# u and y come back in one transfer each, the first conditioning blocks go in four batches, x is split two chunks at a time, powers are built by doubling, and the state inputs move to VectorE

## The reference

```python
mods = (jax.nn.silu(c) @ p['w_ada'] + p['b_ada']).reshape(n, DEPTH, 2, 3, D_MODEL)
h = modulate(x, shift, scale)                 # x * (1 + scale) + shift
u = (h @ w_in).reshape(n, seq, 64, 16)        # 64 groups of 16 channels
a_bar = jnp.exp(lam * dt)                     # 64 complex states a group
b_bar = ((a_bar - 1.0) / lam)[..., None] * lax.complex(b_re, b_im)
bu = einsum('nlgc,gpc->nlgp', u, b_bar)       # bu[:, 0] += a_bar * h0
_, states = lax.associative_scan(_lin_combine, (a_seq, bu), axis=1)
y = gelu(einsum(states, c) + d_skip * u)
z = y @ w_glu
out = z[..., :D_MODEL] * jax.nn.sigmoid(z[..., D_MODEL:])
```

## Time and profile before

| | us |
|---|---|
| median of 3 runs | 2664.37 (2663.33 to 2665.31) |
| the profiled execution | 2662.64 |
| its span in the profile | 2660.8 |
| TensorE busy | 2462.1 (93%) |
| VectorE busy | 1471.5 (55%) |
| GpSimd busy | 1140.3 (43%) |
| ScalarE busy | 626.4 (24%) |
| mean granted TensorE clock | 0.965 of full |

### The profile page before, as it was taken

The page is one execution under the profiler, slowest core; times in us unless marked ns, Lnnn a source line. Parts: engine busy times, 40 slices in busy tenths (PEclk is TensorE's granted clock), DMA queues, the critical chain, the costliest instruction groups (busy, mean ns, idle before and its releaser), DMA issues.

```text
span 2660.8 us, 37232 instructions
## 1 busy us (share of the span) xinstructions
PE 2462.1 (93%) x15472; PEld 2341.2 (88%) x15472; DVE 1471.5 (55%) x2020; ACT 626.4 (24%) x1248; POOL 1140.3 (43%) x604
## 2 busy tenths in 40 slices
PE   5898599879999999999988999987999999999995
PEld 2887499769999999999968999976999999999994
DVE  6998232374565555555574333458555555555555
ACT  4233211143222222122222110103422222222213
POOL 4986234254443434343326333425544444444420
PEclk8999799989999999999999999998999999999998
DMA  6445532102222222112101221100111111111102
GB/s 247 122 125 126 168 111 103 64 16 80 72 80 72 80 79 72 57 63 80 64 32 46 80 72 40 56 25 16 56 48 41 48 48 48 48 48 42 47 24 71
DMA packets 92591, 187.31 MB, mean 70 GB/s; under 512 B 29584, under 2 KB 51856, under 8 KB 92304
## 3 DMA queue, kind: packets, MB, share of 16 engines
q1 hardware_dynamic: 82896, 175.24, 20.2%
q10 hardware_dynamic: 9536, 9.77, 1.0%
HBM read 170.66 MB, written 14.32 MB: 70 GB/s over the span
## 4 chain that ended last, share of the span: by engine, by line
PE 82%; DVE 10%; DVEq 3%; SPq 2%; POOL 1%; ACT 1%; DMA 1%; issue 1%; ACTq 0%
PE bank L628 17%; PE bank L630 17%; PE bank L629 17%; PE bank L838 8%; PE bank L840 7%; PE bank L839 7%; PE bank L857 2%; PE bank L592 1%; DVE X L1627 1%; PE bank L641 1%; SPq L390 1%; DVE ROWS L1619 1%; POOL X L572 1%; DVE X L1613 1%; DVE HL L1655 1%
## 5 line engine op out<-in xcount | busy, mean ns | idle before, releaser
L628 PE MATMUL bank<-HH,WH 128*128 128x344 f32 x2904 | 932.1, 321 | 0.0
L629 PE MATMUL bank<-HL,WH 128*128 128x344 f32 x2904 | 927.6, 319 | 0.0
L630 PE MATMUL bank<-HH,WL 128*128 128x344 f32 x2904 | 927.4, 319 | 0.0
L477 POOL TENSOR_TENSOR WH<-RAW,ZERO 128x1024 fp32r<-128x1024 f32 x176 | 378.6, 2151 | 1198.8 <-DMA RAW<-in_wstream 1164.1
L1593 DVE SCALAR_TENSOR_TENSOR X<-bank,MOD,X 128x344 f32<-128x344 f32 (+1 forms) x624 | 355.4, 571 | 433.2 <-PE bank L840 298.4
L628 PEld LDWEIGHTS bank<-HH,WH 128*128 128x128 f32 x2904 | 545.4, 188 | 15.6 <-issue 14.8
L630 PEld LDWEIGHTS bank<-HH,WL 128*128 128x128 f32 x2904 | 545.8, 188 | 0.0
L629 PEld LDWEIGHTS bank<-HL,WH 128*128 128x128 f32 x2904 | 545.4, 188 | 0.0
L472 POOL TENSOR_TENSOR WL<-RAW,WH 128x1024 fp32r<-128x1024 f32 x188 | 501.7, 2669 | 73.6 <-ACT WH L950 59.8
L838 PE MATMUL bank<-GH,WH 128*128 128x344 f32 x1248 | 410.2, 329 | 22.2 <-DVE X L1593 22.2
L839 PE MATMUL bank<-GL,WH 128*128 128x344 f32 x1248 | 402.8, 323 | 0.0
(11 more groups left out here) (284 smaller groups left out, 2449.6 us busy)
## 6 DMA issues: line engine op xcount, KB each, us to landing
RAW<-in_wstream SPq DMA_DIRECT2D x188, 512.0 KB, 3.5
ADA<-in_wada SPq DMA_DIRECT2D x20, 2048.0 KB, 8.7
FST<-in_wada SPq DMA_DIRECT2D x16, 512.0 KB, 9.9
X<-in_xT SPq DMA_DIRECT2D x1, 4128.0 KB, 17.0
out_yT<-X SPq DMA_DIRECT2D x3, 1376.0 KB, 5.6
FST<-in_xT SPq DMA_DIRECT2D x8, 512.0 KB, 9.1
UT<-s_u SPq DMA_DIRECT2D x64, 64.0 KB, 3.4
s_y<-YG ACTq DMA_DIRECT2D x8, 512.0 KB, 2.8
```

The source lines that it names most:

```text
L477: ptt(WH[:, slot, :], RAW[:, slot, :], bc(ZERO[:, :], [128, 1024]), add).then_inc(s_hi, 1)
L628: pe.matmul(o, wh, hh, start=k == 0, stop=False)
L629: pe.matmul(o, wh, hl, start=False, stop=False)
L630: m = pe.matmul(o, wl, hh, start=False, stop=k == KC - 1)
```

## The change

- `load_u` and `load_y` are one DMA each of 512 KB, in pieces of 512 bytes. For that the partitions hold channel and step in the order (c s) in place of (s c), and y in the order (c g) in place of (g c). So W2 is laid out as (c s) with the powers reversed, TT's rows are strided, the GLU units are loaded with their rows in the new order, and the samples' y is reordered by a matmul with a permuted identity (`order_sample_y`).
- The first 16 conditioning blocks are four batches of the kind that the others are; each is followed on TensorE by a chunk of x. ScalarE adds the bias, GpSimd modulates and splits the samples.
- Low halves of x: chunks 0 to 3 on GpSimd, with the tables between them, chunks 4 to 7 on VectorE.
- The tables are built by doubling from their own last entry; VectorE makes only a^8 of the rotation, and AP_ by doubling too.
- `state_inputs` is VectorE's for all j; `rotations(j)` waits for `chunk_inputs(j-1)`.
- In the tail GLU units 0 and 1 are both computed chunk by chunk (`gate_chunk`), the sample splits are two, outside of `states`, and the batches in the GLU come one unit later.

```diff
-ADA_AT = {n: b + 2 for b, n in enumerate([N_GLU + 1 + 3 * i for i in range(5)]
+ADA_AT = {n: b + 2 for b, n in enumerate([N_GLU + 2 + 3 * i for i in range(5)]
...
+                if N_GLU <= n < N_F0:
+                    src = src.rearrange("(g c) n -> c g n", c=GC)
...
+            def load_first(b):
                 for a in range(2):
+                    sp.dma_start(FST[:, a, 2 * b:2 * b + 2, 0:SEQ],
+                                 wada[8 * a + 2 * b:8 * a + 2 * b + 2, :, :].rearrange("a p n -> p a n")).then_inc(s_first[b], 16)
+            def load_x(k):
+                sp.wait_ge(s_fprod, k // 2 + 1)
+                sp.dma_start(FST[:, 1, k, 0:SEQ], xT[:, k, 0:SEQ]).then_inc(s_xin[k], 16)
+            sp.dma_start(LAM[:, :, :], lam).then_inc(s_lam, 16)
             sp.dma_start(SC[:, :, :], cT).then_inc(s_c, 16)
+            load_first(0)
+            # bada, stack, ident, XS; units 0, 1; x0; H0; first 1; x1; first 2; b; x2, x3; first 3; x4, x5; c...; x6, x7
...
-                for s in range(L):
-                    r = GC * (L - 1 - s)
-                    sp.dma_start(UT[r:r + GC, j % 2], ud[s]).then_inc(s_utl[j % 2], 16)
+                sp.dma_start(UT[:, j % 2], u_dram[j].rearrange("(g c) (s n) -> (c s) g n", c=GC, s=L)).then_inc(s_utl[j % 2], 16)
...
-                    sp.dma_start(TT[r:r + GC, :, GC * s:128], kd[:, :, 0:128 - GC * s]).then_inc(s_tl, 16)
+                    sp.dma_start(TT[s:128:L, :, GC * s:128], kd[:, :, 0:128 - GC * s]).then_inc(s_tl, 16)
...
-                for g in range(8):
-                    sp.dma_start(FST[GC * g:GC * (g + 1), 1, j, 0:SEQ].rearrange("p (s n) -> p s n", s=L), yd[g])\
-                        .then_inc(s_yl[j], 16)
+                sp.dma_start(FST[:, 1, j, 0:SEQ].rearrange("p (s n) -> p s n", s=L),
+                             y_dram[j].rearrange("(s c) (g n) -> (c g) s n", c=GC, g=8)).then_inc(s_yl[j], 16)
...
 (GpSimd)
+            low_half(0); low_half(1)
+            sample_x(0); low_x(0); low_sample_x(0)
+            low_x(1)
+            pool.wait_ge(s_pw, 1)
+            table(LO, 16)
+            sample_x(1); low_x(2); low_sample_x(1)
+            low_x(3)
+            pool.tensor_copy(HI[:, :, :, 1], LO[:, :, :, 16])
+            table(HI, 7)
+            for b in range(2, 4):
+                sample_x(b); low_sample_x(b)
             low_half(2)
             rotations(0)
             low_half(3)
+            for j in range(1, KC):
                 rotations(j)
+                low_half(j + 3)
...
 (TensorE)
+            def first_batch(b):
+                pe.wait_ge(s_first[b], 32)
+                for i in (0, 2, 4, 6, 1, 3, 5, 7):
+                    g = i // 2
+                    m = pe.matmul(BK[6][32 * g:32 * (g + 1), :].rearrange("p (a c n) -> p a c n", a=2, c=2), SCP[:, i, :],
+                                  FST[:, :, 2 * b:2 * b + 2, 128 * i:128 * (i + 1)], start=i % 2 == 0, stop=i % 2 == 1,
                                   skip_group_check=True)
                 m.then_inc(s_fprod, 1)
                 pe.wait_ge(s_fev, b + 1)
+                # four matmuls EVB x STK -> BK[7], then_inc(s_fsum, 1)
+            first_batch(0)
+            pe.wait_ge(s_unit, 2)
+            first_units(0)
+            first_batch(1)
+            first_units(1)
+            first_batch(2)
+            first_units(2)
+            first_batch(3)
+            for k in range(3, KC):
+                first_units(k)
...
 (TensorE, last chunk)
+            order_sample_y(0, KC - 2, 1)
             chunk_inputs(j)
+            pe.wait_ge(s_smp, 1)
             impulse(j)
             for k in range(3):
+                gate_chunk(0, k)
             sample_inputs(j)
             toeplitz(j)
+            for k in range(3, KC - 2):
+                gate_chunk(0, k)
             sample_outputs(j)
             outputs(j)
+            for k in range(KC - 2):
+                gate_chunk(1, k)
+            pe.wait_ge(s_ysd, KC)
+            order_sample_y(KC - 2, KC, 2)
+            for k in range(KC - 2, KC):
+                for u in range(2):
+                    gate_chunk(u, k)
...
 (ScalarE)
+            first_mods(0); high_half(0); high_half(1)
+            high_x(0); high_sample_x(0)
+            first_mods(1); high_x(1)
+            first_mods(2); high_x(2); high_sample_x(1)
+            first_mods(3); high_x(3)
+            high_x(4); high_sample_x(2)
+            high_x(5); high_sample_x(3)
+            high_x(6); high_x(7)
...
 (VectorE)
+            state_inputs(0)
+            for k in range(4, KC):
+                low_x(k)
             output_matrix(0)
+            state_inputs(1)
             for j in range(KC):
                 states(j)
                 if j < KC - 1:
                     output_matrix(j + 1)
                 sample_y(j)
+                if j < KC - 2:
+                    state_inputs(j + 2)
                 if j == KC - 2:
                     sample_split(0, KC - 2, 1)
-            sample_split(KC - 1, KC, 3)
+            sample_split(KC - 2, KC, 2)
```

More of the change, by code:

```diff
@@ L140, in trunk_kernel @@
         IDN = sb("IDN", [128, 128], F32, early)
-        SC = sb("SC", [128, KC, 9], F32, early)
+        IDNP = sb("IDNP", [128, 128], F32, early)
         RHO = sb("RHO", [128, NP_], F32, early)
@@ new lines, in _ @@
+            sp.dma_start(H0[:, :, :, :], h0T).then_inc(s_h0l, 16)
+            load_first(1)
+            load_x(1)
+            load_first(2)
+            for i in range(2):
+                sp.dma_start(BR[:, i], bT[i]).then_inc(s_cst4, 16)
+            load_x(2)
+            load_x(3)
+            load_first(3)
+            load_x(4)
+            load_x(5)
+            for dst, src in ((CR[:, 0], cS[0]), (CR[:, 1], cS[1]), (DSK[:, :], dT), (E16[:, :], eye16), (PM[:, :, :], pmask)):
+                sp.dma_start(dst, src).then_inc(s_cst2, 16)
@@ L360, in _ @@
+            load_x(6)
+            load_x(7)
             load_unit(2)
@@ L495, in product, with table @@
                 return ptt(out[1], t[0], t[1], add)
-            def tables():
-                pool.wait_ge(s_pw, 1)
-                for t, levels, lv0 in ((LO, 4, 0), (HI, 3, 4)):
-                    for lv in range(levels):
-                        m = 1 << lv
-                        u = [bc(UP7[:, pl, lv0 + lv, :].unsqueeze(2), [128, NP_, m]) for pl in range(2)]
-                        product([t[:, pl, :, m:2 * m] for pl in range(2)], [t[:, pl, :, 0:m] for pl in range(2)], u, (NP_, m))
-                        pool.drain()
+            def table(t, count):
+                m = 1
+                while m < count:
+                    w = min(m, count - m)
+                    u = [bc(t[:, pl, :, m:m + 1], [128, NP_, w]) for pl in range(2)]
+                    product([t[:, pl, :, m + 1:m + 1 + w] for pl in range(2)], [t[:, pl, :, 1:1 + w] for pl in range(2)], u, (NP_, w))
+                    pool.drain()
+                    m += w
@@ L536, in _ @@
             low_half(1)
-            tables()
-            for k in range(KC):
-                low_x(k)
+            sample_x(0)
+            low_x(0)
+            low_sample_x(0)
+            low_x(1)
+            pool.wait_ge(s_pw, 1)
+            table(LO, 16)
+            sample_x(1)
+            low_x(2)
+            low_sample_x(1)
+            low_x(3)
+            pool.tensor_copy(HI[:, :, :, 1], LO[:, :, :, 16])
+            pool.drain()
+            table(HI, 7)
+            for b in range(2, 4):
+                sample_x(b)
+                low_sample_x(b)
             low_half(2)
@@ L542, in _ @@
             low_half(3)
-            pool.wait_ge(s_bb, 1)
-            state_inputs(1)
-            rotations(1)
-            for j in range(2, KC):
-                low_half(j + 2)
-                state_inputs(j)
+            for j in range(1, KC):
                 rotations(j)
+                low_half(j + 3)
             for k in range(KC - 1):
-                if k == 3:
-                    low_half(KC + 2)
                 low_y(k)
```

290 lines of the change are left out of this document (152 added, 138 removed).

## The result

| | before | after |
|---|---|---|
| median of 11 runs each, us | 2664.98 (2659.39 to 2668.84) | 2672.93 (2668.46 to 2676.16) |
| the profiled execution (span) | 2662.64 (2660.8) | 2669.78 (2667.8) |
| TensorE busy | 2462.1 | 2452.7 |
| mean granted TensorE clock | 0.965 | 0.961 |

The ratio after to before is 1.0028, 95% interval 1.0019 to 1.0037: slower by 7.5 us, where 12 us faster was forecast. 2672.9 lies above the range, and the difference is more than the 5.3 us that the forecast took for no change.

A forecast was written before the change was run, and what follows sets the result against it. It saw the movable time in the first 334 us, with TensorE waiting at the start and tail and alternating with VectorE in the loop. +4 + 17.5 - 33.6 = -12 us gave 2652 us, range 2630 to 2668.

The forecast's parts named there:

- Part 2: S5 loop: state inputs on VectorE meet GpSimd's rotations, passes 25.2 us against 22.3, +17.5 us over six passes.
- cover the state inputs in every pass: Loop: rotations begin at the end of output_matrix and meet the state inputs each pass, making it 25.2 us.
- rival B: Loop: rotations stay inside the states, whose PSUM operands do not collide; loop -3 us, whole 2632; chance 0.25.
- A: The forecast itself, with the rotations covering the state inputs in the loop: whole at 2643 to 2660 us; chance 0.45.
- Part 1: Start, batches and chunks of x: rounds of 14.5 us, states(0) at 107.6 against 103.4, +4 us, bounds -6 and +10.
- Part 3: Tail, u and y in one transfer each: states(6) to both gate units -35.1 us, -33.6 with unit 2's batch.
- the term behind it: After the gate units: unit 2's batch waits for ScalarE to empty the banks of unit 0, +1.5 us.
- y7 has to follow the 4.2 MB of X ... landed 291: Tail: the last y load queues behind X, 17.0 us to landing; landed 291, split 293.4, in time before.
- rival C: u and y transfers: 1024 pieces are slow as one; 2.4 us longer each cancels the gain, 10 gives 2680; chance 0.14.
- a sign of being wrong: Tail transfers: the forecast is wrong if a y load lands after more than 8 us; landing expected at 4 to 5.
- The sum: Whole kernel: +4 for the start, +17.5 for the loop, -33.6 for the tail, together -12 us, to 2652.

The follow-up runs named there:

- b1: Kernel before with only the state inputs of chunks 1 to 7 moved to VectorE, rotations(j) started by chunk_inputs(j-1); ratio 1.0071 to the kernel before.
- e1: Changed kernel with one wait replaced, so rotations(j) on GpSimd start with states(j-1) on VectorE; ratio 0.9913 to the kernel before.
- e3: Changed kernel with GpSimd's samples of pairs 2 and 3 ahead of the second table; ratio 0.9977 to the kernel before.
- e7: Changed kernel with all four conditioning batches before the first x chunk, and GpSimd's low halves and samples before both tables; ratio 0.9938 to the kernel before.
- e9: Changed kernel with GLU unit 1 computed after unit 0, all its chunks behind the last y chunk; ratio 1.0070 to the kernel before.
- e4: Changed kernel with the residual X loaded after the last y chunk and not before it; ratio 1.0017 to the kernel before.
- e5: Changed kernel with GpSimd's low halves of y held back until VectorE's last output matrix is done; ratio 1.0011 to the kernel before.
- e11: Changed kernel with the edits of e3, e4 and e5 together, loop left as it is; ratio 0.9935 to the kernel before.
- e6: Changed kernel with u and y back in eight transfers of 64 KB each; ratio 1.0062 to the kernel before.
- e12: Changed kernel with the edits of e7, e1, e5 and e4, rotations(0) ahead of low_half(2), and low_half(2) on VectorE; ratio 0.9822 to the kernel before.

## Why the prediction was wrong

**Part 2, the loop: right in mechanism, the size in part by luck.** 17.7 us against 17.5. State inputs took 1.40 to 1.77 and the sixth 2.67 where they met the rotations, and b1 shows 15.9 us more in the loop without the rest of the change. But "cover the state inputs in every pass" did not hold: the passes lie between 22.6 and 27.4, with all six operations met in two of them, four in two, and one in the two with a conditioning batch. Their mean is the 25.2 of the forecast because the errors cancel. By the Trainium skill ("SBUF — State Buffer", section "SBUF: two separate sides") the ports are an exclusive lock for whole instructions, not a share: the row of 2.80 us at 281.54, 0.76 of its own work behind a low half that takes 2.35 alone, agrees. The forecast's rival B was this same part with another start of the rotations; the code named the start (`s_e`), so A over B was the right choice, and e1 measured B's pass: 20.8 against 21.0.

**Part 1, the start: +14.7 against +4, the term that left its bounds.** The rounds were right (15.1 against 14.5, first matmul 26.6 against 25.5). The step that failed is the price of the work between them. The first table was priced as it ran in the kernel before, 12.3. VectorE worked beside it there too, but almost only on operations of 32 elements; the change puts operations of 256 and 512 elements there, and it took 16.3. So round 2 began at 61.5 and not 55.5. The second table took 9.2 with a copy in front of it that the forecast has no price for, against 7.2, and ScalarE's wait for the sample rows behind it ended at 85.9 and not 78. VectorE began `output_matrix(0)` at 94.4 and not 86.8: 7.6 of the miss of 10.5 us at `states(0)`. Output matrix 0 and state inputs 1, given 10 and 9, took 10.7 and 10.3, which is 2.0 more; the rest is in the small operations between and behind them, for which the forecast lists 1 us, though its sum has 1.8. The order on GpSimd was seen and not judged: e3 shows that four small operations in front of the second table are worth 14 us, and e7 that this and all batches ahead of x are worth 24 together.

**Part 3, the tail: -23.9 against -35.1** (with the term behind it, -25.4 against -33.6). Right in what went (the sample split, y in ScalarE's way) and in the fill of unit 1 (e9). Two steps failed. "y7 has to follow the 4.2 MB of X ... landed 291" counted the load's place in SyncE's queue and not the store that it waits for, which runs beside X and takes 10.4 us (4.1 in e4); and the meeting of output matrix 7 with the low halves was priced +3 where it was +6. Without them the time from states(6) to the gate units is 6.1 us shorter (e4), 5.6 (e5) and, with e3, 11.3 (e11), about as much as the gap of 11.2. A third price was low as well: a transfer landed in 6.3 (u) and 7.0 us (y) in the median, not 4.4. That is 1.9 and 2.6 more, about the 2.4 at which rival C has the gain gone, and short of its 3.5 for a clear loss; one y load, behind 2 MB of conditioning weights, took 11.0, past the 8 that the forecast named as a sign of being wrong. What these landings cost in the whole no run shows, nor which price of the tail was too high to make up for them; e6 shows only that eight transfers are no better. No row shows the 2.0 us of latency that the 4.4 contains. By the fit of the Trainium skill ("DMA: Bandwidth & Descriptors", section "Anatomy of one DMA"), which that page gives for transfers issued by GpSimd and not by SyncE, it would be an estimated 3.2 for 512 KB; no single transfer of u or y in the changed kernel landed in under 4.1, so the measurement decides.

**The sum.** Much of both misses has one cause: durations of the kernel before were used for work that the change makes simultaneous (the first table, the store beside X, output matrix 7). The loop was the one term for which the price under collision was worked out for a whole pass. The range ended at 2668, which is the start's upper bound, the loop as forecast and the tail's -24, together (+3.5); the start lay 4.7 us beyond its bound, while the tail with the term behind it lay 1.4 inside its own. With three small edits the changed kernel is 17 us faster than the kernel before (e11), with those of e12 47.

## What to carry to other kernels

When a change moves work between VectorE and GpSimd, list what will run at the same moment on the other one, and put GpSimd's SBUF work beside VectorE operations that have an operand in PSUM; here the place of one wait was worth 31 us. Put small operations that another engine waits for in front of long ones on the same queue. A load that waits for a store inherits what runs beside the store (10.4 us here with X, 4.1 without).

## What the runs showed of the hardware

- Small operations can wait many times their own length: the copy of 128x8 at 280.12 took 1.33 us in the changed kernel, with a low half of y on GpSimd since 279.1, and 0.17 in e1 and e5. It has one input in SBUF, so it is not only operations with two that wait, as the forecast read its rows. X's scaling (one input too) took 2.88 us at 330.9 in e5, beside a low half that GpSimd began at 330.7, and 0.70 in e4.
- A transfer of 1024 pieces takes SyncE 0.46 us (u) and 0.59 us (y) to issue in the median, not the 1.1 of XS at the start; single issues took up to 3.1.
- TensorE's mean granted clock from states(0) to states(6) was 0.95 before, 0.90 in the changed kernel, where it stands still for 22.0 of 151.3 us, and 0.99 in e1, with 8.1 of 127.1.
